# One transfer of 1 MB per ring buffer in place of two of 512 KB, in the weight stream of a decoder step

## The reference, cut to what matters

```python
def ada_modulation(c, w_ada, b_ada):              # w_ada: 2048 x 12288
    m = jax.nn.silu(c) @ w_ada + b_ada
    return jnp.split(m[:, None, :], 6, axis=-1)

h = rms_norm(x, g_pre) * (1.0 + scale) + shift
z = h @ w_in                                      # 2048 x 4096: q, k, v, u
q, k, v, u = jnp.split(z, [1024, 2048, 3072], axis=-1)
attn = diff_attend(rotary(q), rotary(k), v, ...)  # 8 heads; the samples also read paged K and V
pooled = pool_mix(u, ...)                         # windows of 2, 4, 8, 16 rows, then w_pool
m = jnp.concatenate([rms_norm(attn, g_subln) * (1.0 - lam_init), pooled], axis=-1) @ w_out
x = x + gate * rms_norm(m, g_post)
h = rms_norm(x, g_pre_ffn) * (1.0 + scale2) + shift2
f = jnp.square(jax.nn.relu(h @ w1)) @ w2          # 2048 x 8192 and 8192 x 2048
x = x + gate2 * rms_norm(f, g_post_ffn)
```

## Time and profile before

| | us |
|---|---|
| median of three runs | 1468.08 |
| the profiled execution | 1467.77 |
| its span, first to last instruction | 1466.1 |
| TensorE busy | 1433.8 |
| VectorE busy | 814.9 |
| ScalarE busy | 524.8 |
| GpSimd busy | 115.4 |

### The profile page before, as it was taken

The page is one execution under the profiler, slowest core; times in us unless marked ns, Lnnn a source line. Parts: engine busy times, 40 slices in busy tenths (PEclk is TensorE's granted clock), DMA queues, the critical chain, the costliest instruction groups (busy, mean ns, idle before and its releaser), DMA issues.

```text
span 1466.1 us, 26898 instructions
## 1 busy us (share of the span) xinstructions
PE 1433.8 (98%) x10278; PEld 1316.6 (90%) x10278; DVE 814.9 (56%) x1312; ACT 524.8 (36%) x753; POOL 115.4 (8%) x195
## 2 busy tenths in 40 slices
PE   6999999999999999999999999999999999999996
PEld 2788877888688879999999999999999999999996
DVE  5667668757555678664434554343554334555554
ACT  4333243443435644333222333332333322333331
POOL 1111000266210000000000000000000000000002
PEclk9999999999999999999999999999999999999998
DMA  9999888787799777334346334446443443334421
GB/s 374 342 340 341 331 311 314 276 310 281 282 349 347 280 269 300 144 143 172 143 165 238 144 143 157 159 144 239 156 151 144 152 161 146 144 143 144 149 109 72
DMA packets 88459, 319.06 MB, mean 218 GB/s; under 512 B 12240, under 2 KB 12496, under 8 KB 87744
## 3 DMA queue, kind: packets, MB, share of 16 engines
q1 hardware_dynamic: 79776, 290.49, 53.4%
q0 software_dynamic: 5360, 25.14, 4.6%
q10 hardware_dynamic: 3248, 2.39, 0.5%
HBM read 312.18 MB, written 5.80 MB: 217 GB/s over the span
## 4 chain that ended last, share of the span: by engine, by line
PE 93%; DVE 3%; DMA 1%; POOL 1%; issue 1%; ACT 1%; SPq 0%; POOLq 0%; ACTq 0%; DVEq 0%
PE bank L1572 74%; PE bank L1625 8%; PE bank L1549 3%; PE bank L1534 2%; PE bank L1897 2%; DMA raw<-in_stream 1%; PE bank L1812 1%; DVE w_lo L812 1%; PE bank L1743 1%; PE bank L1559 0%; PE bank L1842 0%; PE bank L1698 0%; PE bank L1524 0%; SPq L371 0%; ACT w_hi L418 0%
## 5 line engine op out<-in xcount | busy, mean ns | idle before, releaser
L418 ACT ACTIVATE w_hi<-raw 128x1024 fp32r<-128x1024 f32 x352 | 361.6, 1053 | 271.8 <-PE bank L1572 232.0
L812 DVE TENSOR_TENSOR w_lo<-raw,w_hi 128x1024 fp32r<-128x1024 f32 x352 | 419.6, 1226 | 40.9 <-ACT w_hi L418 38.6
L1572 PE MATMUL bank<-m_hi,w_hi 128*128 128x320 f32 x1280 | 397.2, 310 | 0.0
L1572 PE MATMUL bank<-m_hi,w_lo 128*128 128x320 f32 x1280 | 395.5, 309 | 0.0
L1572 PE MATMUL bank<-m_lo,w_hi 128*128 128x320 f32 x1280 | 395.5, 309 | 0.0
L1572 PE MATMUL bank<-h_hi,w_hi 128*128 128x320 f32 x1216 | 378.7, 311 | 0.0
L1572 PE MATMUL bank<-h_hi,w_lo 128*128 128x320 f32 x1216 | 375.7, 309 | 0.0
L1572 PE MATMUL bank<-h_lo,w_hi 128*128 128x320 f32 x1216 | 375.7, 309 | 0.0
L1572 PEld LDWEIGHTS bank<-m_hi,w_hi 128*128 128x128 f32 x1280 | 240.3, 188 | 12.0 <-issue 12.0
L1572 PEld LDWEIGHTS bank<-h_hi,w_hi 128*128 128x128 f32 x1216 | 228.3, 188 | 13.9 <-issue 13.8
L1572 PEld LDWEIGHTS bank<-m_lo,w_hi 128*128 128x128 f32 x1280 | 240.3, 188 | 0.0
(11 more groups left out here) (240 smaller groups left out, 1130.3 us busy)
## 6 DMA issues: line engine op xcount, KB each, us to landing
raw<-in_stream SPq DMA_DIRECT2D x544, 512.0 KB, 4.3
k_pages<-in_kc POOLq DMA_DIRECT2D x16, 512.0 KB, 6.4
v_pages<-in_vc POOLq DMA_DIRECT2D x16, 512.0 KB, 5.4
x<-in_x_cm SPq DMA_DIRECT2D x4, 640.0 KB, 6.8
x_mid<-in_x_cm POOLq DMA_DIRECT2D x1, 2560.0 KB, 10.0
x<-in_x_cm POOLq DMA_DIRECT2D x1, 2560.0 KB, 13.8
v_out<-v_cm POOLq DMA_DIRECT2D x1, 1280.0 KB, 9.5
k_out<-back POOLq DMA_DIRECT2D x1, 1280.0 KB, 6.0
```

What stands on the lines that cost most here:

```text
L418: act.activation(w_hi[2 * (j % 2) + h][:, :], raw[slot][:, h * 1024:(h + 1) * 1024], ACT.Copy).then_inc(hi_ready, 1)
L812: dve.tensor_tensor(w_lo[q][:, :], raw[slot][:, h * 1024:(h + 1) * 1024], w_hi[q][:, :], ALU.subtract).then_inc(slot_used[slot], 1)
L1572: last = pe.matmul(bank[j % 2][:, 0:T], w[q][:, k * P:(k + 1) * P], v[:, 8 * h + k, :], start=(h == 0 and k == 0 and n == 0), stop=(h == 1 ...
```

## The change

SyncE issues one transfer of 128 x 2048 per buffer, with rows of 8 KB in the buffer and in the stream, where it issued two of 128 x 1024 with rows of 4 KB. It increments one semaphore per buffer, `raw_loaded[s]`. All readers of either half wait for it. The host packs a chunk as it is, without the split into two halves. Nothing else changes, and every engine keeps its order of work.

```diff
-    raw_loaded = [[S(f"raw_loaded{s}_{h}") for h in range(2)] for s in range(4)]
+    raw_loaded = [S(f"raw_loaded{s}") for s in range(4)]
...
                 sp.wait_ge(slot_used[s], 2 * i + 2)
-                for h in range(2):
-                    half = slice(h * 1024, (h + 1) * 1024)
-                    sp.dma_start(raw[s][:, half], stream[ds(4 * i + s, 1), h, :, :].rearrange("a p n -> p (a n)")).then_inc(
-                        raw_loaded[s][h], 16)
+                sp.dma_start(raw[s][:, :], stream[ds(4 * i + s, 1), :, :].rearrange("a p n -> p (a n)")).then_inc(
+                    raw_loaded[s], 16)
...
         def hi_half(c4, use, off, j, h):
             slot, u = use_of(use, off)
-            act.wait_ge(raw_loaded[slot][h], 16 * (u + 1))
+            act.wait_ge(raw_loaded[slot], 16 * (u + 1))
...
             for kk in range(4):
-                if kk % 2 == 0:
-                    pe.wait_ge(raw_loaded[slot][kk // 2], 16 * (u + 1))
+                if kk == 0:
+                    pe.wait_ge(raw_loaded[slot], 16 * (u + 1))
...
             for g in range(4):
-                if g % 2 == 0:
-                    pe.wait_ge(raw_loaded[slot][g // 2], 16 * (u + 1))
+                if g == 0:
+                    pe.wait_ge(raw_loaded[slot], 16 * (u + 1))
...
-    return np.ascontiguousarray(np.stack(chunks).reshape(STREAM, P, 2, 1024).transpose(0, 2, 1, 3))
+    return np.ascontiguousarray(np.stack(chunks))
```

## The result

The changed kernel takes 1471.75 us, the median of 12 executions (1469.78 to 1475.48), against 1468.07 us for the kernel before, the median of 12 (1466.61 to 1471.46). The ratio is 1.0032, 95% interval 1.0025 to 1.0039: slower, by 3.7 us by the medians and 4.7 us by the ratio. The prediction was +0.7 us. Of the runs behind all these figures, one execution of one_start (3661.61 us) and one of the kernel before (4955.36 us) are left out of the ratios and of the mean clocks.

What follows compares the result with a forecast made beforehand. TensorE was taken as the bound (busy 1433.8 of 1466.1 us), with the stream setting the pace only in the first 40 us. Terms -0.5 + 0.0 + 0.2 + 1.0 = +0.7 gave 1468.8 us, range 1466.8 to 1471.8.

Steps and rivals of the forecast that it cites:

- Start, -0.5: 0 to 40 us: 8 KB rows land the 20th half 0.8 us earlier, of which TensorE gains 0.5 us.
- rival (b): Start: longer idles lower TensorE's clock, 1.5 us worse than forecast, 1470.3 us; chance 0.11.
- 40 to 180 us, 0: Modulation slices, 40 to 180 us: buffers still land before TensorE takes them, so no time is lost.
- The slack of 0.7 us: Last modulation buffer of a slice: complete at 94.0 us, taken by TensorE at 94.8; five such slices.
- rival (a): 1 MB lands after the old second half's time: 1470.7 us at 0.9 lag, 1474.9 at 1.6 (slices late); chance 0.12.
- Attention, +0.2: 195 to 250 us: a later first-half conversion delays the first head; 0 to 1.8 us lost, 0.2 taken.
- 0.9 us fit into the first: Attention: TensorE's first later idle for a rotated q, up to 1.3 us, was to absorb a 0.9 us delay.
- the load of the pool state: Attention: GpSimd's load was to come about 1.3 us later, letting the whole buffer through before it, at about 199.6 us.
- Norm, +1.0: 540 to 568 us: a later first-half conversion delays h_lo for TensorE; 0 to 1.5 us lost, 1.0 taken.
- MLP, 0: MLP: buffers land far ahead of their use, so nothing changes.
- (c): Each transfer's fixed cost is paid now, so half as many transfers save 8 us: 1460.1 us; chance 0.04.
- The estimate of 20 us won: Start: ten fixed parts of 2.0 us fewer before 40 us, by the skill page; the prediction rejected it.

Runs made afterwards that it cites:

- one_start: Kernel before with whole 1 MB transfers on one semaphore in the ring's first 13 turns (to about 190 us), halves elsewhere; 1467.52 us, ratio 1.0005.
- after_reordered: Changed kernel with first-half conversions put behind the work they held up, at the first attention head and in the norm; 1470.19 us, ratio 1.0015 to before.
- one_attention: Kernel before with whole 1 MB transfers in turns 13 to 29 of the ring only, halves elsewhere; 1470.11 us, ratio 1.0015.
- turn15_whole: Kernel before with whole 1 MB transfers in turn 15 of the ring alone (4 of 272 chunks); 1469.46 us, ratio 1.0007.
- few_whole: Kernel before with whole 1 MB transfers in turns 0 to 2, 15 and 34 only, halves in the other 63; 1470.52 us, ratio 1.0014.
- both_waited: Kernel before with its two transfers and two semaphores per buffer, but every reader of either half waits for both; 1472.69 us, ratio 1.0036.
- after_kept: Changed kernel with more matmuls that only keep TensorE busy, filling the start's waits for whole buffers; 1470.41 us, ratio 1.0016 to before.
- one_norm: Kernel before with whole 1 MB transfers in turns 30 to 35 of the ring only, halves elsewhere; 1469.68 us, ratio 1.0012.
- one_mlp: Kernel before with whole 1 MB transfers from turn 35 of the ring to the end, halves ahead of it; 1467.59 us, ratio 1.0000.
- few_halved: Changed kernel with halves and two semaphores in turns 0 to 2, 15 and 34 only; 1469.03 us, ratio 1.0016 to before.

## Why the prediction was wrong, point by point

*Start, -0.5.* The transfer side was right. Rows of 8 KB bring 3% (2.48 us in place of 2.56), the bank additions become a link of the chain, and one_start's profile ends this phase 0.9 us sooner, within the bounds of 0 to 1.2. Two steps failed. One is the choice against rival (b), at 0.11. TensorE's idles on the stream, 0.15 to 1.27 us before, are mostly near 1.4 us and up to 3.0, and the granted clock falls to half in every profile of the kind but the filled one, for 3.4 or 6.8 us, somewhere from 21 to 37 us. Where this meets the products it costs: the changed kernel's profile ends the phase 1.9 us late (the rival had 1.5 over the forecast), after_reordered's 0.8. Where the fall ends by 27 us, as in one_start, it costs nothing that shows. So the term spreads from -0.9 to +1.9 us between profiles; one_start as a kernel measured +0.7 by the ratio. The other step is that the terms were added as if a gain in the start stayed: in one_start TensorE waits 0.8 us for the rotated q at 210 us, and 0.2 of the 0.9 us are left. The late rise to full speed in the changed kernel is no cause: one_attention, whose start has halves, has it as well (two matmuls at 15.29 us take 1.44 us, as in the changed kernel at 15.38, against 0.81 before) and ends the phase at 40.06.

*40 to 180 us, 0.* Right: 140.00 of 140.00 us busy. The slack of 0.7 us held, and rival (a) in its dear form fell.

*Attention, +0.2: the step that failed most.* Two parts of it are wrong. "0.9 us fit into the first" idle: TensorE's later waits for a rotated q are not room that a delay fills. They move along with the delay, unshortened (269.79 in turn15_whole against 268.86, 1.27 us both); in the changed kernel both are still there and a third has been added (3.8 us in three against 2.4 in two). And the load of the pool state mostly did not come later: in turn15_whole, few_whole and one_attention GpSimd issues it at 194.2 to 194.5 us, as in the earlier trace rows, and in the changed kernel at 196.23, later only by the 1.9 us of its start, so the whole buffer is behind it as the second half was. In both_waited it was 0.4 us later (194.95), in after_kept 1.1 (195.65). The buffer's landing, 4.8 to 6.1 us after the issue, spans nearly the width of my bounds, and even at the early one, 199.6, TensorE lost 1.1 us where I had 0. For the late one, 201.4, I had 1.8; one_attention, at 201.0, lost 2.4. As a kernel it measured +2.2 us.

*Norm, +1.0.* The mechanism is right and the size was too small. One_norm measured +1.8 us by the medians; its profile, one of the two fastest of its 11 executions, has 0.8 us of new waits for h_lo, where the conversion waited 2.85 us for the stream instead of 1.36. In the changed kernel's profile the transfer took 6.98 us, where I had let the whole buffer land when the old second half did, 5.4 us after the first half's issue: this is rival (a), but at one place. With TensorE's wait of 2.5 us goes a fall of the clock to half, which costs 1.3 more. The prediction had no term for a fall outside the start.

*MLP, 0.* Nothing speaks against it: one_mlp at 1.0000 (0.9990 to 1.0009).

*The whole.* Three errors of one sign, by the ratios: start 0.7 instead of -0.5, attention 2.2 instead of 0.2, norm 1.8 instead of 1.0. They make 4.0 us, the distance from +0.7 to +4.7. The range of 1466.8 to 1471.8 just holds the median, and that is luck: it was stretched for (a), (b) and (c), while the attention alone went past its bound of 1.8. The chance of slower, 0.13, was far too low. The attention, bounded from 0 upwards, was taken near its lower end. The Trainium skill, "DMA: Bandwidth & Descriptors", section "Bandwidth", advises transfers of at least 1 MiB. The estimate of 20 us won took the fixed 2.0 us per transfer from that page's section "Anatomy of one DMA — SWDGE (gpsimd) path", which is fitted to transfers issued by GpSimd; the stream is issued by SyncE. The runs do not bear either out for this kernel: halves and whole buffers move 1 MB in 2.56 us alike (rows of 4 KB), and both_waited shows what the second semaphore was worth, 4.9 us by the medians.

*What stays open.* Why the whole transfer of turn 15 lands 4.8 us after its issue in turn15_whole and 6.1 in one_attention, with the pool state's load at the same moment. And which of the 63 other turns make few_halved slower than before. Its trace shows 0.4 us near 234 us, at the rotated q of a later head, and four of its 11 executions are above 1471 us with a lower clock, which no profile caught. Two other profiles point to the later heads too: at 259 us TensorE waits 1.2 us for a rotated q in both_waited and 0.9 in after_kept, where the kernel before has no such wait. Open too is what the fall of the clock alone costs in the start.

## What to carry to other kernels

A second semaphore on half a buffer is worth keeping where an engine converts the first half ahead of work that others wait for; look for that order first, and count the delay in full unless the idle behind it is set by something that the delay does not move. Where the tensor engine lives on landings, larger pieces make longer idles, and the clock can cost more than the transfers save. When most terms of a sum can only go one way, put the forecast in the middle of the bounds, not at their quiet end; and do not carry a gain in one stage through a later stage that waits for the same stream.

## What the runs showed of the hardware

Like idles of TensorE bring the clock down once and not the next time. In one_attention waits of 0.97 and 1.43 us, at 211 and 213 us, are followed by the lower of its two levels (1.2 of 2.4 GHz), as the window shows (columns as above):

```profile
213.60:217.00 3.40, 3.40 (x15) 2.91 (x12) 3.33 (x11) 0.46 (x3) 0.46 (x1) 0.50 1.04 436
```

In the changed kernel nearly the same pair is not. The rows of the latter, at full speed:

```profile
212.59 0.55 PE L1710 MATMUL bank<-tab,probs 128*128 128x128 f32 x3 [0.66 <-DVE probs L964]
214.57 0.93 PE L1696 MATMUL bank<-back 64*128 64x128 f32 x8 [1.43 <-DVE back L909]
215.42 0.42 PE L1570 MATMUL bank<-h_hi,w_hi 128*128 128x320 f32 x1
215.68 0.31 PE L1570 MATMUL bank<-h_lo,w_hi 128*128 128x320 f32 x1
```

Also unexpected: the kernel's own matmuls for the clock, 20 more of about 0.22 us (14 in a row take 3.29 us), cost nothing that shows when they lie in waits, and in the start, with rows of 4 KB, a transfer of 1 MB takes the queue as long as two of 512 KB, 2.56 us.
